# Twelve expert rows a head beside the routing, ten behind it; the second token set turned inside the gates; the value rows begun in the scores

## The reference, cut to what matters

```
q = (x @ w_query).reshape(NT, 8 heads, 2, 128)
s = q . sub_keys                      # 8 heads x 2 x 128 scores for each token
v1, i1 = top_k(s[:, :, 0], 16); v2, i2 = top_k(s[:, :, 1], 16)
best, ci = top_k(v1[..., :, None] + v2[..., None, :], 16)      # 16 of 256
idx = e1 * 128 + e2                   # 16384 experts, 128 (8 x 16) for each token
gate = softmax(best)
act = gelu(x . expert_u[idx]);  y = sum over the 128 of (gate * act) * expert_v[idx]
out = rms_norm(h + y)
```

## Time and profile before

| | us |
|---|---|
| median of 3 runs (lowest, highest) | 4124.49 (4123.36, 4125.99) |
| time of the profiled execution | 4125.52 |
| its span (first to last instruction) | 4123.8 |
| PE busy | 3999.3 |
| DVE busy | 2356.7 |
| POOL busy | 2303.3 |
| ACT busy | 1350.0 |

### The profile page before, as it was taken

One profiled execution on the slowest core, in us unless ns is written; L12 is line 12 of the kernel. 1 busy time (PEld: TensorE's weight loads), 2 busy tenths in 40 slices (PEclk: granted clock), 3 DMA queues, 4 the chain that ended last, 5 costly groups with the idle time before them and its releaser, 6 DMA issues.

```text
span 4123.8 us, 67398 instructions
## 1 busy us (share of the span) xinstructions
PE 3999.3 (97%) x27585; PEld 3579.7 (87%) x27585; DVE 2356.7 (57%) x3478; ACT 1350.0 (33%) x1388; POOL 2303.3 (56%) x930
## 2 busy tenths in 40 slices
PE   7999999999999999989999999999998999999997
PEld 5777777777778787879999999999998999999997
DVE  4343344443464554147777757776436777777675
ACT  4323233223232221133323334444223333333333
POOL 4332323332333344435666656666767899998884
PEclk9999999999999999989999999999999999999998
DMA  3222222222232344235666659989888999999992
GB/s 116 100 78 87 80 88 88 85 86 85 78 106 96 120 144 150 100 121 218 268 252 257 253 200 353 352 343 350 333 336 314 378 384 378 382 390 368 329 382 102
DMA packets 258449, 900.18 MB, mean 218 GB/s; under 512 B 107672, under 2 KB 140696, under 8 KB 162736
## 3 DMA queue, kind: packets, MB, share of 16 engines
q1 hardware_dynamic: 175984, 482.50, 33.1%
q0 software_dynamic: 46080, 335.56, 20.1%
q10 hardware_dynamic: 36160, 78.85, 4.9%
HBM read 828.10 MB, written 68.71 MB: 217 GB/s over the span
## 4 chain that ended last, share of the span: by engine, by line
PE 85%; POOL 4%; DMA 4%; DVE 3%; issue 2%; ACT 1%; SPq 1%; ACTq 0%; DVEq 0%; POOLq 0%
PE ps L417 20%; PE ps L419 19%; PE ps L418 19%; PE ps L2011 6%; PE ps L2013 6%; PE ps L2012 6%; PE ps L1690 2%; PE ps L1964 2%; POOL wl L408 2%; DMA raw<-stream 1%; DMA rowb<-v_rows,idx 1%; POOL wl L412 1%; SPq L583 1%; ACT wh L393 1%; PE ps L1842 0%
## 5 line engine op out<-in xcount | busy, mean ns | idle before, releaser
L412 POOL TENSOR_TENSOR wl<-raw,wh 128x2048 fp32r<-128x2048 f32 x268 | 1243.5, 4640 | 1585.9 <-ACT wh L393 1585.9
L417 PE MATMUL ps<-xh,wh 128*128 128x352 f32 (+1 forms) x3904 | 1439.8, 369 | 43.0 <-POOL wl L412 21.4
L419 PE MATMUL ps<-xh,wl 128*128 128x352 f32 (+1 forms) x3904 | 1398.4, 358 | 0.0
L418 PE MATMUL ps<-xl,wh 128*128 128x352 f32 (+1 forms) x3904 | 1397.4, 358 | 0.0
L417 PEld LDWEIGHTS ps<-xh,wh 128*128 128x128 f32 x3904 | 738.2, 189 | 142.0 <-issue 49.0
L393 ACT ACTIVATE wh<-raw 128x2048 fp32r<-128x2048 f32 x270 | 516.7, 1914 | 938.8 <-PE ps L419 850.1
L419 PEld LDWEIGHTS ps<-xh,wl 128*128 128x128 f32 x3904 | 737.2, 189 | 83.5
L418 PEld LDWEIGHTS ps<-xl,wh 128*128 128x128 f32 x3904 | 738.4, 189 | 81.7 <-issue 7.7
L2011 PE MATMUL ps<-gah,wh 128*128 128x352 f32 x2048 | 666.2, 325 | 24.6 <-POOL wl L408 14.6
L2013 PE MATMUL ps<-gah,wl 128*128 128x352 f32 x2048 | 663.2, 324 | 0.0
L2012 PE MATMUL ps<-gal,wh 128*128 128x352 f32 x2048 | 660.6, 323 | 0.0
(11 more groups left out here) (330 smaller groups left out, 3937.5 us busy)
## 6 DMA issues: line engine op xcount, KB each, us to landing
raw<-stream SPq DMA_DIRECT2D x396, 1024.0 KB, 4.9
gelu_scratch<-preb ACTq DMA_DIRECT2D x128, 176.0 KB
gates_scratch<-stage ACTq DMA_DIRECT2D x22, 1024.0 KB, 8.8
gt<-gates_scratch SPq DMA_DIRECT2D x32, 704.0 KB, 11.9
act<-gelu_scratch SPq DMA_DIRECT2D x32, 704.0 KB, 16.4
mergegate_scratch<-sgb ACTq DMA_DIRECT2D x32, 256.0 KB, 2.0
sgm<-mergegate_scratch SPq DMA_DIRECT2D x32, 256.0 KB, 2.7
h_in<-x_t SPq DMA_DIRECT2D x4, 1024.0 KB, 9.6
```

What stands on the lines that cost most here:

```text
L412: pool.tensor_tensor(wl[s][:, :], raw[s][:, :], wh[s][:, :].bitcast(F32), ALU.subtract).then_inc(w_lo, 1)
L417: pe.matmul(dst, w_h, h[:, kx, lo:], start=start, stop=False)
L418: pe.matmul(dst, w_h, l[:, kx, lo:], start=False, stop=False)
L419: return pe.matmul(dst, w_l, h[:, kx, lo:], start=False, stop=stop)
```

## The change

- **Heads.** `EARLY` goes from 8 to 12 rows a head (84 rows in all), in five buffers instead of four; buffer 0 is the first quarter of `H` until `J_BACK`, which is also where the tokens wait to be turned (`xd`), so POOL waits for the turning (`xg_ready`) before its first fetch. The four further rows of a head are used by DVE two after selection c = 0 and two after selection c = 1 of the next head (`EARLY_KEYS`), ahead of the next `idx`. The fetches stand behind units 2 (two), 3 (three), 4, 5, 7 (two each) and unit 1 of the head after (one).
- **Tail.** `TAIL` = 10 more rows: fetched two each behind the tail's units m = 2 to 6, used by DVE after the end of head 7 and before it copies `iota_ps` and makes the first one-hots.
- **Gates.** The last 34 rows of the first set are fetched in j = 0 to 17 (before: 72 rows in j = 2 to 50). DVE rebuilds `xd` for the second set at j = 18 and PE turns it after unit 19 (before: in the rest, after unit 52). The 32 rows of the second set are fetched in j = 20 to 49 (before: j = 52 to 77).
- **The rest of the scores.** At j = 50 to 52 DVE clears `xg`, ACT makes the GELU and DVE `coef` (before: after value group 1, behind `dve_values`). 23 `v` rows are fetched in j = 51 to 68 and 5 in 69 to 73 (before: none).
- **Values.** 100 `v` rows in j = 74 to 158 (before: 128 in j = 79 to 166), the last 32 in 31 units of groups 22 to 30 (before: in 19 units of groups 24 to 29). `W_GROUP` goes from 25 to 23, and `save_sums` for the second set moves into group 30, behind its third unit.

```diff
-R_TURNED, V_GROUP, W_GROUP = 4, 2, 25
+J_TURN, W_GROUP = 20, 23
-EARLY = 8
+EARLY, TAIL = 12, 10
-EARLY_AT = {2: (0, 1), 3: (2, 3), 4: (4,), 5: (5,), 6: (6,), 7: (7,)}
-EARLY_NOW, EARLY_NEXT = range(0, 4), range(4, EARLY)
+EARLY_AT = {1: (-1,), 2: (0, 1), 3: (2, 3, 4), 4: (5, 6), 5: (7, 8), 7: (9, 10)}
+EARLY_NOW, EARLY_KEYS, EARLY_NEXT = range(0, 4), ((4, 5), (6, 7)), range(8, EARLY)
-MORE = 24
-FETCHED_AT.update({n: -1 for n in range(EARLY_ALL)})
-fetches(EARLY_ALL, SLOTS - EARLY_ALL, range(2, F_GATES + R_TURNED - 1), 0)
-fetches(SLOTS, MORE, range(F_GATES + R_TURNED, J_BACK), F_GATES + R_TURNED + 1)
...
+J_V, NOW = 50, 23
+FIRST = EARLY_ALL + TAIL
+FETCHED_AT.update({n: -1 for n in range(FIRST)})
+fetches(FIRST, SLOTS - FIRST, range(0, J_TURN - 2), 0)
+fetches(SLOTS, ALL - SLOTS, range(J_TURN, J_V), J_TURN + 1)
+fetches(ALL, NOW, range(J_V + 1, J_BACK), J_V + 3)
...
-    homes = range(1, ROWS) if n < EARLY_ALL else range(ROWS_LOW if J_BACK <= FETCHED_AT[n] < J_HIGH else ROWS)
+    homes = range(ROWS_LOW if J_BACK <= FETCHED_AT[n] < J_HIGH else ROWS)
...  POOL, the heads and the tail
                         if i == 0:
                             pool.wait_ge(sets_ready, h + 1)
-                        fetch(EARLY * (h - 1) + i)
-            for n in range(U_ROUTED, score_unit(SC_GATES)):
+                            pool.wait_ge(xg_ready, 1)
+                        if EARLY * (h - 1) + i >= 0:
+                            fetch(EARLY * (h - 1) + i)
+            for m, n in enumerate(range(U_ROUTED, score_unit(SC_GATES))):
                 split_lo(pool, n, n % 2)
+                for i in EARLY_AT.get(m, ()):
+                    if i < 0:
+                        fetch(EARLY_ALL + i)
+                if 2 <= m < 2 + TAIL // 2:
+                    for i in range(2):
+                        fetch(EARLY_ALL + 2 * (m - 2) + i)
...  ACT, the rest of the scores
+                if r == J_V - F_GATES + 1:
+                    act.wait_ge(row_used, ALL)
+                    act.activation(gel[:, :], dots[:, :], ACT.Gelu).then_inc(gel_ready, 1)
...  DVE, the heads
                     dve.sem_inc(sel_done, 1)
                     if h and c == 0:
                         weights(h - 1)
+                    for i in EARLY_KEYS[c] if h else ():
+                        use(EARLY * (h - 1) + i)
...  DVE, behind head 7
+            for n in range(EARLY_ALL, FIRST):
+                use(n)
             dve.wait_ge(egt_saved, 3)
             own(dve, dve.tensor_copy(iota_ps, iota128[:, :]), sets_ready, HEADS + 3)
...  DVE, the gates and the rest of the scores
+                if j == J_TURN - 2:
                     dve.wait_ge(row_used, SLOTS)
                     for q in range(SETS):
                         last = dve.tensor_tensor(xd[:, :, G2 * q:G2 * q + G2], xh[:, :, P:G].bitcast(F32), xl[:, :, P:G].bitcast(F32), ALU.add)
                     last.then_inc(sets_ready, 1)
+                if j == J_TURN:
+                    dve.wait_ge(xg_ready, 2)
...
+                if r == J_V - F_GATES:
+                    dve.wait_ge(row_used, ALL)
+                    dve.memset(xg, 0.0)
...
-            for g in range(V_GROUP):
-                dve_values(g)
-            dve.wait_ge(row_used, ALL)
-            dve.memset(xg, 0.0)
-            dve.wait_ge(gel_ready, 1)
-            step(dve.tensor_tensor(coef[:, :], gel[:, :], gate0[:, :], ALU.mult))
-            for g in range(V_GROUP, W_GROUP):
+            for g in range(W_GROUP):
                 dve_values(g)
...  PE
-            with pe.Fori(1, GATES_TWO // 2) as i:
+            with pe.Fori(1, J_TURN // 2) as i:
+                for s in range(2):
+                    gates_two(2 * i + s, s)
+            turn(HEADS + 4)
+            with pe.Fori(J_TURN // 2, GATES_TWO // 2) as i:
...
-                if r == R_TURNED:
-                    turn(HEADS + 4)
```

More of the change, by code:

```diff
@@ L305, in build @@
         sb("gates_gap", [P, 4 * OH * P + N])
-        rows_low = [sb(f"rowb{b}", [P, D]) for b in range(ROWS_LOW)]
+        rows_low = [sb(f"rowb{b}", [P, D])[:, :] for b in range(ROWS_LOW)]
         while len(stack) > 1:
@@ L706, in _ @@
                 for n in FETCHED[j]:
-                    if n == EARLY_ALL:
-                        pool.wait_ge(sets_ready, HEADS + 3)
+                    if n == FIRST:
+                        pool.wait_ge(sets_ready, HEADS + 1)
+                    if n == SLOTS:
                         pool.wait_ge(routing_in, 16 + 16 * 2 * SETS)
-                        pool.wait_ge(oh_ready, 1)
+                    if n >= SLOTS and j < J_BACK and ROW_AT[n] == 0:
+                        pool.wait_ge(xg_ready, 2)
+                    if j >= J_BACK:
+                        pool.wait_ge(gates_stored[1], 16 + 8 * GB)
                     fetch(n)
@@ L1074, in act_gates @@
                               stage[s][:, :, :].rearrange("p e t -> p (e t)")).then_inc(gates_stored[s], 16)
-            with act.Fori(0, GATES_TWO // 4) as b:
+            act.wait_ge(routing_in, 16 + 16 * 2 * SETS)
+            per = GT // OH
+            with act.Fori(0, GATES_TWO // per) as b:
                 for s in range(2):
-                    act_gates(2 * b + s, s, 2, 2 * (2 * b + s))
-            with act.Fori(GATES_TWO // 4, GB // 2) as b:
+                    act_gates(2 * b + s, s, per // 2, per // 2 * (2 * b + s))
+            with act.Fori(GATES_TWO // per, GB // 2) as b:
                 for s in range(2):
-                    act_gates(2 * b + s, s, 4, 4 * (2 * b + s) - GATES_TWO)
+                    act_gates(2 * b + s, s, per, per * (2 * b + s) - GATES_TWO)
             def act_halves(g, s, e):
@@ L1102, in _, with act_values @@
                         act_halves(0, 0, e)
-            def act_values(g, s, ahead=AHEAD):
+            def act_values(g, s, ahead=AHEAD, then=None):
                 for c in range(NC4):
@@ L1108, in act_values @@
                     value_hi(act, NC4 * g + c + 2)
-            for g in range(V_GROUP):
+                    if then and c == 2:
+                        then()
+            for g in range(W_GROUP - 1):
                 act_values(g, g % 2, AHEAD if g else AHEAD_1)
[L1112 to L1115, removed]
             def save_sums(used):
@@ L1125, in _ @@
             act.wait_ge(sum_out, 4)
-            save_sums(2 * ALL)
-            act_values(GROUPS - 2, 0)
+            act_values(GROUPS - 2, 0, then=lambda: save_sums(2 * ALL))
             gain = lambda d: par[:, C_GAIN + 2 * KT + d:C_GAIN + 2 * KT + d + 1]
@@ L1548, in _ @@
                     use(n)
-            for r in range(F_REST):
-                if r == R_TURNED + 1:
-                    dve.wait_ge(xg_ready, 2)
-                for n in USED[F_GATES + r]:
-                    use(n)
-                if r == R_TURNED - 1:
-                    for s in range(2):
-                        dve.wait_ge(gates_stored[s], 16 + 8 * GB)
+                if j == J_TURN - 2:
                     dve.wait_ge(row_used, SLOTS)
@@ L1560, in _ @@
                     last.then_inc(sets_ready, 1)
+                if j == J_TURN:
+                    dve.wait_ge(xg_ready, 2)
+            for r in range(F_REST):
+                if r == J_V - F_GATES + 2:
+                    dve.wait_ge(gel_ready, 1)
+                    step(dve.tensor_tensor(coef[:, :], gel[:, :], gate0[:, :], ALU.mult))
+                for n in USED[F_GATES + r]:
+                    use(n)
+                if r == J_V - F_GATES:
+                    dve.wait_ge(row_used, ALL)
+                    dve.memset(xg, 0.0)
                 if r == R_GATED:
+                    for s in range(2):
+                        dve.wait_ge(gates_stored[s], 16 + 8 * GB)
                     for e in range(GE):
                         dve_low(0, 0, e)
-            for g in range(V_GROUP):
-                dve_values(g)
-            dve.wait_ge(row_used, ALL)
-            dve.memset(xg, 0.0)
-            dve.wait_ge(gel_ready, 1)
-            step(dve.tensor_tensor(coef[:, :], gel[:, :], gate0[:, :], ALU.mult))
-            for g in range(V_GROUP, W_GROUP):
+            for g in range(W_GROUP):
                 dve_values(g)
```

11 lines of the change are left out of this document (4 added, 7 removed).

## The result

| | before | changed |
|---|---|---|
| median of 6 runs (lowest, highest), us | 4124.86 (4119.04, 4132.3) | 4139.43 (4134.81, 4143.02) |
| profiled execution: time; span, us | 4125.52; 4123.8 | 4143.02; 4141.0 |
| PE at the transposes of the gates, us from the start | 2410.60 | 2437.62 |
| from there to the end of the span, us | 1713.2 | 1703.4 |

The changed kernel is slower: the ratio is 1.0034, 95% interval 1.0022 to 1.0047, so 9 to 19 us. The span grew by 17.2 us: 27.0 us were lost up to the gates' transposes, and 9.8 us won behind them. The profiled execution lies 3.6 us over its median, the one of before 0.7 over its own; that is why the medians are only 14.6 us apart.

The account below looks back on a forecast made before the run. PE, busy 97% of the span, was taken as the bound. Routing +38, gates +1 and gains -17 made +22 us, moving the median from 4124.5 to 4146; own range 4137 to 4156, 8 in 10 within 4110 to 4160.

Parts of the forecast that it names:

- The routing: Heads and tail together, up to the gates' transposes: 37 to 40 us lost, taken as 38.
- DVE sets the heads' period: Heads: 8.84 us more DVE work against 4.4 free, so heads 74.8 us apart instead of 70.33.
- Tail: After head 7: row 89's fetch awaits the first tail row, delaying a split; PE ends m = 5 at 2447.2 to 2450.8.
- The sign in the heads: Changed profile, heads: PE would show waits of 1 to 5 us in each late head.
- the one in the tail: Changed profile, tail: PE would show two waits of 10 us or more.
- Gates: +1: First 18 gates units: added rows load the DMA and cost 0 to 2 us, taken as 1.
- its upper case: Gates: a loss of 5.7 us over 18 units if 384 GB/s were the DMA's end.
- The gains: Behind 2870 us: 17 won, from `coef` 6.4, splits 3, the first sum 6.9, scattered waits 1.
- `H` coming back and a group load ahead of a unit's weights: untouched.: Last scores and first value groups: these make the other 7.9 us of PE's waits, which stay.
- 1 (absorbed): Heads: DVE's lag is absorbed and PE never waits there; 4108 us, chance 0.13.
- 2 (half of it, 18 us): Heads and tail: PE's margins and fewer row waits hold the lag to some 18 us; 4126 us, chance 0.12.
- 3: First 18 gates units bound by DMA, or moved rows bring nothing behind 2870 us; 4152 to 4158 us, chance 0.11.

Follow-up runs that it names:

- Experiment 1: The changed kernel with the four further rows a head multiplied over 64 of their 2048 columns only, fetches unchanged; 4115.28 us, ratio 0.998.
- experiment 2: The changed kernel with ten rows a head instead of 12, eight in the tail, the rows left over moved to the gates; 4119.94 us, ratio 0.9993.
- experiment 8: The kernel before, with the reciprocals that `weights` multiplies by in PSUM instead of SBUF; one execution, 4115.41 us.
- experiment 4: The changed kernel with the nine `v` rows of units 69 to 76 spread over the value units from 77 on; 4125.56 us, ratio 1.0003.
- experiment 5: Three variants of the changed kernel: four rows of units 74 to 76, five of 69 to 73, or one of 74 moved later; ratios 1.0024, 1.001, 1.002.
- experiment 6: The kernel before with its 32 second-set rows all in units 52 to 68, none in 69 to 77; 4121.72 us, ratio 1.0002.

## Why the prediction was right, and where its terms were off

The forecast was 4146 us and the median is 4139.4. Direction and cause stand. Two sizes were off: the routing cost 27.0 us and not 38, and the stages behind it gave back 9.8 and not 16. These errors cancel in part, so that the total came nearer than its terms is luck.

- **DVE sets the heads' period: right, 74.8 us mis-sized, 73.0 measured.** Experiment 1 shows the cause, experiment 2 about where it sets in, and the 2.21 us of a use held. The term that was off is DVE's own work. In the kernel before, `EG` lasts 1.2 to 1.6 us in each of these heads, held by a split; I had counted that as work. In heads 2 to 7 of the changed kernel it lasts 0.22 or 0.23: at 2146.57 it is between two splits (2144.99 to 2148.21). I read that as the split now following DVE, since POOL waits for `idx`; no run tests it. `ex` was held in two heads instead, by 2.1 and 1.2 us. Unheld, a head takes 72.9 us, so the overrun is 2.6 us a head, not 4.4. Of the 1.9 us between 74.8 and 72.9 the freed `EG` is 1.25; another 0.3 is free time, which is 4.7 us in the mean and not 4.4; the last 0.3 I haven't placed. (The Trainium skill, SBUF — State Buffer, SBUF: two separate sides, has the rule: a DVE instruction with two SBUF inputs and a GpSimd one that reads SBUF exclude each other. The traces agree: the held steps of experiment 8 end within 0.1 us of the split. The prediction used the rule only to fear more holds, but here a hold went away.)
- **Tail: right in its steps.** From `idx` of head 7 to the end of `sel` it took 19.1 us, the low end of 19.1 to 22.7. The first tail row, the fetch of row 89, the split and the unit followed as worked out, except that PE's wait there was 0.88 us and not over 10, and cost no clock (granted 1.00 from 2429 to 2433 us). The clock fell behind the wait at 2410.86 instead (granted 0.50, the lower level, from 2411 to 2415). **The routing cost 27.0 us, not 38**; 8.3 of the 11 us between are the earlier `idx` of head 7. The sign in the heads held, with one longer wait of PE of 1.6 to 1.9 us in each; the one in the tail was wrong, 5.05 and 0.88 us instead of two of 10 or more.
- **Gates: +1, nothing seen.** PE has no wait between 2450 and 2870 us. (A slip in the prediction: 3.74 MB at 384 GB/s take 9.74 us, so its upper case was 5.2 us, not 5.7; the sum doesn't use it.)
- **The gains: 17 forecast, some 12 by the pauses.** Adding up what PE's matmuls take beyond 0.16 us each at every pause, before and after: `coef` 5.7 -> 0 (forecast 6.4 won), the first sum 8.5 -> 3.4 (forecast 6.9, got 5.1), scattered ones in the values 4.1 -> near 0 (forecast 1). But up to unit 64 it is 10.4 -> 10.4 (forecast 3 won), and at the first value units 13.7 -> 16.9. The sum of these is 5.7 + 5.1 + 4 + 0 - 3.2 = 11.6; the spans show 9.8 won, and the other 2 us (the turning inside the gates among them) I haven't placed.
- **The step that failed: "`H` coming back and a group load ahead of a unit's weights: untouched."** The wait is neither made by these alone (experiment 4: without row fetches it is zero) nor untouched (7.9 -> 11.8). The diff put two fetches behind unit 74 where one was, since 100 rows over 85 units put two into the first, and moving the second away took 2.5 us off the wait (experiment 5). Of the growth, 1.6 us are no more than what two executions of the old schedule differ by.
- **Rivals.** 1 (absorbed) fell: DVE has no wait left to absorb with, and experiment 1, where it has, is 22 us faster. 2 (half of it, 18 us) was too low, though the 27.0 measured lie nearer to it than to 38; its reason, that PE's margins swallow the lag, isn't what was found, since the smaller loss is in DVE's own chain. 3 fell for the gates; that the moved rows bring less behind 2870 us was partly true.

## What to carry to other kernels

Read an engine's free time in the period of the loop you load, not in the span: here some 4.5 us in 70.3, while the page says 57% busy; two more uses a head just about fill it (70.8 us), four cost PE 2.6 us each time, through a fetch that stands ahead of a split. When a wait for a load is found, look at what else is in flight at that time, not only at that load: taking nine gathers from beside the group loads was worth 13 us when they went to the value units (experiment 4); moving eight in the kernel before to a stretch that was then at a DMA share of 0.97 won nothing (experiment 6). And a short step that lasts several times its usual time in each round can be a wait in disguise: look at what ends with it before counting it as work, and expect it back elsewhere when the phase shifts. Last, compare a single wait over two traces of the same schedule before explaining a few microseconds of it (7.9 and 9.5 us here).

## What was not expected of the hardware

- A DVE step of 0.2 us with both inputs in SBUF ended with POOL's 4.6 us `tensor_tensor` wherever it started inside it (1.6, 1.0, 2.0 us above); with one input in PSUM it didn't (0.22 us). Removing one such hold moved it to the next such step. The rebuilding of `xd`, four `tensor_tensor` from SBUF, took 2.49 us in the changed kernel, where it started between two splits, and 6.49 before, where it started inside one (2903.52 to 2908.15).
- With one 1 MB gather less just ahead of the activations' load, PE's wait was 2.5 us shorter in one trace. That is about what 1 MB takes at the 383 GB/s of the changed kernel from 3110 to 3130 us (2.7 us, an estimate), as if the load came by so much later; but executions of one schedule differ there by up to 1.6 us.
